# Group 4 of the modulation weights: from TensorE products to VectorE sums, behind the attention units of a fused transformer front

## The reference

```python
sc, sc_ctx = silu(c), silu(c_ctx)
for i in range(2):
    m  = (sc     @ w_mod[i] + b_mod[i]).reshape(1, 6, 1024)   # w_mod[i]: 1024 x 6144
    mc = (sc_ctx @ w_mod[i] + b_mod[i]).reshape(6, 1024)
    sh1, s1, g1, sh2, s2, g2 = ...                            # used as x * (1 + s1) + sh1, and so on

merged = sigmoid(g_a) * (out_a @ w_proj_a) + sigmoid(g_b) * (out_b @ w_proj_b)
mix = merged @ w_out
x = layer_norm(ALPHA * x + mix)          # then the router and the experts
```

## Time and profile before

| what | value |
|---|---|
| median of 3 runs | 3478.19 us (3475.61 to 3481.51) |
| profiled execution | 3470.34 us, span of the profile 3468.5 us |
| TensorE busy | 3156.0 us (91%), mean granted clock 0.985 |
| VectorE, ScalarE, GpSimd busy | 1831.5 us (53%), 1130.2 us (33%), 882.6 us (25%) |
| transfers | 1366.35 MB, mean 394 GB/s |
| chain that ended last | indirect row transfers 10%, TensorE 9%, VectorE 2% of the span |

### The profile page before, as it was taken

How to read it: one execution, slowest core, us unless ns; L and a number is a source line. 1 busy time by engine, 2 the same in 40 slices (tenths; PEclk the granted TensorE clock), 3 DMA queues, 4 the chain that set the end, 5 groups by cost and what they waited for, 6 DMA issues and landing times. The chain is left out here.

```text
span 3468.5 us, 33334 instructions
## 1 busy us (share of the span) xinstructions
PE 3156.0 (91%) x11076; PEld 1414.2 (41%) x11076; DVE 1831.5 (53%) x4099; ACT 1130.2 (33%) x3024; POOL 882.6 (25%) x798
## 2 busy tenths in 40 slices
PE   9999999999999997989989879889888998987777
PEld 7565333433334432434344323333333643532222
DVE  7743102111221127676776677667765378667665
ACT  1331111110111113444443544555433334444333
POOL 0000000000000003444444444345442034444432
PEclk9999999999999999999999999999999999999999
DMA  9847999999999999999999999999998379999997
GB/s 406 362 175 297 425 425 428 425 423 428 417 427 427 401 427 399 410 422 419 417 421 413 421 411 422 413 412 415 416 421 343 127 309 421 422 421 418 420 421 331
DMA packets 155595, 1366.35 MB, mean 394 GB/s; under 512 B 18341, under 2 KB 18853, under 8 KB 24090
## 3 DMA queue, kind: packets, MB, share of 16 engines
q0 software_dynamic: 111360, 805.46, 56.2%
q1 hardware_dynamic: 44058, 558.70, 38.5%
HBM read 1362.94 MB, written 1.15 MB: 393 GB/s over the span
## 5 line engine op out<-in xcount | busy, mean ns | idle before, releaser
L3423 PE MATMUL ps<-sb_arena,sb_diag 128*128 128x512 f32 x3072 | 1472.7, 619 | 259.4 <-ACT sb_diag L3402 257.4
L1910 POOL DMA_INDIRECT sb_arena<-in_uv,sb_idx x768 | 866.2, 1128 | 2165.1 <-PE ps L3423 1035.5
L3358 DVE SCALAR_TENSOR_TENSOR sb_arena<-sb_arena,sb_H 128x1024 f32<-128x1024 f32 x768 | 941.0, 1226 | 583.5 <-DMA sb_arena<-in_uv,sb_idx 399.2
L3423 PEld LDWEIGHTS ps<-sb_arena,sb_diag 128*128 128x128 f32 x3072 | 563.5, 194 | 1117.6 <-ACT sb_diag L3402 557.6
L1571 PE MATMUL ps<-sb_ring,sb_arena 128*64 128x512 f32 x3072 | 675.2, 595 | 7.4 <-DMA sb_ring<-in_moe 7.4
L3391 ACT ACTIVATE sb_act<-sb_dots 128x1 f32<-128x1 f32 x768 | 154.8, 202 | 998.2 <-DVE sb_arena L3358 993.3
L1571 PEld LDWEIGHTS ps<-sb_ring,sb_arena 128*64 128x64 f32 x3072 | 214.1, 137 | 447.0 <-issue 429.6
L1772 DVE TENSOR_SCALAR sb_arena<-ps 128x512 f32<-128x512 f32 x32 | 22.1, 692 | 585.3 <-PE ps L1571 569.9
L3402 ACT ACTIVATE sb_diag<-sb_consts,sb_act 128x128 f32<-128x128 f32 x768 | 308.4, 402 | 26.1 <-PE ps L3423 1.2
L3397 ACT ACTIVATE sb_act<-sb_act,sb_wts 128x1 f32<-128x1 f32 x768 | 226.2, 295 | 25.0
L183 PE MATMUL ps<-sb_ring,sb_arena 128*128 128x512 f32 x256 | 111.4, 593 | 1.6 <-DVE sb_arena L857 1.3
(11 more groups left out here) (444 smaller groups left out, 2595.5 us busy)
## 6 DMA issues: line engine op xcount, KB each, us to landing
sb_ring<-in_moe SPq DMA_DIRECT2D x192, 2048.0 KB, 17.1
sb_ring<-in_w_mod SPq DMA_DIRECT2D x24, 2048.0 KB, 15.2
sb_ring<-in_w_in SPq DMA_DIRECT2D x10, 2048.0 KB, 15.4
sb_ring<-in_a_w_in SPq DMA_DIRECT2D x8, 2048.0 KB, 14.6
sb_ring<-in_w_q SPq DMA_DIRECT2D x6, 2048.0 KB, 12.7
sb_arena<-in_uv,sb_idx POOLq DMA_INDIRECT x768, 14.4
sb_ring<-in_b_w_in SPq DMA_DIRECT2D x6, 2048.0 KB, 7.8
sb_ring<-in_a_w_out SPq DMA_DIRECT2D x4, 2048.0 KB, 14.4
```

The source lines that it names most:

```text
L1910: pool.indirect_dma_start(row_buffer(m, n), None, d[f"uv{layer}"], bass.IndirectOffsetOnAxis(m.idx[:, pair % 2, k:k + 1], 0))\
L3358: nc.vector.scalar_tensor_tensor(out=u, in0=u, scalar=1.0, in1=m.H[:, order[i], :], op0=ALU.mult, op1=ALU.mult, accum_out=m.dots[:, n_ % P ...
L3423: last = nc.tensor.matmul(out[h], m.diag[n_ % DIAGS], uv[b][:, D + h * 512:D + (h + 1) * 512], start=opens, stop=ends)
```

## The change

Group 4 goes to VectorE. `SUMMED_QUARTERS` becomes a table with all four quarters of group 4 in it. Its two sums lie in the part of the arena that held queries, keys and values ("behind"). `add` becomes a generator, `added`, which stops after every instruction, so that its 16 instructions can be put between others: VectorE runs five steps of it after the last attention unit (the first quarter and one instruction), one after each of the first seven merged tiles, and the last four behind the eighth. TensorE drops `mod.tensor(pe, MOD_END)` ahead of the projections and runs `mod.reduce(pe, MOD_END)` between x1 and x2. The group's bank is now 3 and not 4, ScalarE's copy of it comes behind the first square root of the norm, and SyncE waits for the full bank before it loads the expert biases, whose place overlaps one of the sums.

```diff
@@ -36,7 +36,7 @@
...
 N_MOD = 2 * 6 * D // (4 * 512)
 LATE_MODS = 1
-SUMMED_QUARTERS = (4, 4, 3)
+SUMMED_QUARTERS = {0: 4, 1: 4, 2: 3, 4: 4}
 MOD_FILL, MOD_END = 3, 4
@@ -280,7 +280,11 @@
...
         self.sums = [[m.part(7168, 2048), m.part(9216, 2048)],
                      [m.X[:, 0:2, :].rearrange("p a b -> p (a b)"), m.H[:, 2:4, :].rearrange("p a b -> p (a b)")]]
-        self.where, self.adds = {}, 0
+        self.behind = [m.part(2048, 2048), m.part(5120, 2048)]
+        self.where, self.adds, self.summed = {}, 0, {i: n + 1 for n, i in enumerate(SUMMED_QUARTERS)}
+
+    def sums_of(self, i):
+        return self.behind if i == MOD_END else self.sums[i % 2]
@@ -305,17 +309,21 @@
...
     def add(self, dve, i, quarter):
+        for _ in self.added(dve, i, quarter):
+            pass
+
+    def added(self, dve, i, quarter):
...
         if i == 0 and quarter == 0:
             dve.wait_ge(M("silu_ready"), 1)
-        if i >= 2 and quarter == 0:
+        if i == 2 and quarter == 0:
             self.banks.wait_full(dve, self.where[i - 2])
...
         for k in range(2):
             for stream in range(2):
-                out, scale = self.sums[i % 2][stream], self.silu_c[:, 2 * quarter + k, stream:stream + 1]
+                out, scale = self.sums_of(i)[stream], self.silu_c[:, 2 * quarter + k, stream:stream + 1]
                 if self.adds >= 2:
@@ -324,10 +332,13 @@
...
                 ins.then_inc(M("mod_add"), 1)
                 self.adds += 1
+                if k == 0 or stream == 0:
+                    yield
         dve.wait_ge(M("mod_add"), self.adds)
...
         if quarter == SUMMED_QUARTERS[i] - 1:
             dve.sem_inc(M("mod_summed"), 1)
+        yield
@@ -341,12 +352,12 @@
...
                                             w[:, k, g * 512:(g + 1) * 512], start=False, stop=False, skip_group_check=True)
             self.ring.used(last, name)
-        pe.wait_ge(self.M("mod_summed"), i + 1)
+        pe.wait_ge(self.M("mod_summed"), self.summed[i])
         select = m.const("stream").rearrange("p (s c) -> p s c", s=2)
...
             for g in range(4):
                 last = nc.tensor.matmul(m.ps[32 * g:32 * g + 2, where[0], :], select[:, stream, :],
-                                        self.sums[i % 2][stream][:, g * 512:(g + 1) * 512], start=False, stop=stream == 1,
+                                        self.sums_of(i)[stream][:, g * 512:(g + 1) * 512], start=False, stop=stream == 1,
                                         skip_group_check=True)
@@ -443,12 +454,12 @@
...
     mod.plan([MOD_FILL], [7])
     gg.update(banks.plan([("gate", n) for n in range(2, 8)], [7]))
-    mod.plan([MOD_END], [4])
     pieces = [("gate", n, third) for n in range(8) for third in range(3)]
...
     gm = banks.plan([("m", i) for i in range(KT)], [0, 1, 2, 3, 5, 6, 7, 4])
     gx = banks.plan([("x", i) for i in range(4)], [4, 5, 6, 7])
+    mod.plan([MOD_END], [3])
     router = Router(nc, d, m, M, banks)
@@ -487,6 +498,7 @@
...
             ring.load(sp, ring.at["moe0.0"] + 2)
             sp.wait_ge(M("y_ready"), 2 * TT)
+            banks.wait_full(sp, mod.where[MOD_END])
             router.rest(sp)
@@ -645,7 +657,6 @@
...
-            mod.tensor(pe, MOD_END)
             wa = ring.wait(pe, "w_proj_a", 0)
@@ -668,6 +679,8 @@
...
             for i in range(4):
                 t, half = i // 2, i % 2
+                if i == 2:
+                    mod.reduce(pe, MOD_END)
                 w = ring.wait(pe, "w_out", half)
@@ -762,11 +775,10 @@
...
                     gates_out(n)
             for i in range(4):
-                if i == 2:
-                    mod.scalar(act, MOD_END)
                 for n in (i, 4 + i):
                     nc.scalar.activation(pair_of(n), pair_of(n), ACT.Sigmoid).then_inc(M("gates_ready"), 1)
             norm_act(nc, act, m, M, n0 + 1)
+            mod.scalar(act, MOD_END)
             router.turned(act, 0)
@@ -848,6 +860,9 @@
...
             both = m.part(7168, 2, KT, T)
+            behind = (step_ for quarter in range(4) for step_ in mod.added(dve, MOD_END, quarter))
+            for _ in range(5):
+                next(behind)
             for i in range(KT):
@@ -856,6 +871,10 @@
...
                 nc.vector.tensor_tensor(gates[:, i, :], tmp[:, 0, :], tmp[:, 1, :], ALU.add).then_inc(M("merged_ready"), 1)
                 dve.wait_ge(M("merged_ready"), i + 1)
+                if i + 1 < KT:
+                    next(behind, None)
+            for _ in behind:
+                pass
             dve.wait_ge(M("x_in"), 16)
```

## The result

The changed kernel takes 3481.22 us (median of 20 runs, 3473.76 to 3487.47), the kernel before 3477.31 us in the same comparison (20 runs). The ratio is **1.0016, 95% interval 1.001 to 1.0022**: 3.5 to 7.7 us slower, 5.6 in the middle (the two medians lie 3.9 us apart). The forecast was 1.3 us slower, range -5 to +8. Direction and range held, and the ratio is within the 0.2% that counted as no change; the size forecast was a quarter to a third of the measured one.

The account below looks back on a forecast made before the run. TensorE paces the front; at 424.7 us the nearly full weight stream decides. TensorE gains 8.3, pays 2.9, loses the remaining 5.4 and 1.3 more; 1.3 on the median of 3478.19 gives 3479.5 us, range 3473 to 3486.

Parts of the forecast that it names:

- C, the clock: After TensorE's pause ahead of the first turn the clock falls: 1.9 us, up to 5.3 at both waits; 3482, chance 0.12.
- The removed and added TensorE time: Ahead of the projections 8.3 us go, reduce between x1 and x2 adds 2.9; TensorE has 5.4 us less to do.
- VectorE in step with the tiles: In the merge, tile plus accumulating instruction takes 3.5 us, as TensorE's tile does; w_out starts 7.4 us earlier.
- the ring's hidden loads: Weight loads waiting for VectorE's quarters: w_proj_b's second half hidden by 5.6 us, w_out's second half just in time.
- The rows behind three chunks: The layer norm's rows queue behind w_mod20 to w_mod22, 6 MB, and land at 298.6 in place of 281.9.
- What is late next: Before the first expert: second normalized tile at 311.4, 1.9 us late; first expert 0.5 to 1.5 us later than 322.49.
- The stream: Weight transfers behind w_mod20: moe0.2 lands at 322.1 against 320.8, 1.3 us late, and the stream is full until 424.7.
- A cover of 2.6 us: Near 425 us, a wait of 1.25 us plus the stream's 1.3 absorbs TensorE's own lateness of 0.5 to 1.5.
- a first wait for expert chunks that is gone: Sign of being wrong; the forecast had this wait near 425 us still there, ending near 426.
- Rivals A and B: A: rows in time, 5.4 us reach the end, 3472.8, chance 0.1. B: queue shares bandwidth, rows at 306.5, 3486, chance 0.06.
- Theory 3: Put up for the experiments, not in the prediction: VectorE's sums have a cost that no wait shows; no size given.

Follow-up runs that it names:

- e1: Changed kernel with the layer norm's rows issued at about 232 us, ahead of everything that waits for the sums; ratio 1.0001 to the kernel before.
- e9: Changed kernel with the layer norm's rows issued right behind the wait for the merged tiles, ahead of w_mod20 to w_mod22; ratio 1.0003 to the kernel before.
- e3: Changed kernel with four extra products filling TensorE's pause between x3 and its first turn; ratio 1.0012 to the kernel before.
- e4: Kernel before, with the layer norm's rows, router_w, router_b and ctx issued early; ratio 0.9996 to the kernel before.

## Why the prediction was right, and what it mis-sized

The forecast said that TensorE's 5.4 us are lost on the late rows and the late weights, and a little more; that happened. Its time, 3479.5, held because the range was wide and 0.2% counted as no change: both prices in it were too small, that of TensorE's lateness at the first expert and that of the stream's, and of its cases C, the clock, with 3482 and a chance of 0.12, lies closest to what the traces show.

*The removed and added TensorE time.* 8.3 and 2.9 us: removed as said; reduce took 1.04 and 1.90. But TensorE was only 3.8 us ahead at x3, not 4.7 (299.7 for 304.4): w_out started at 269.36 and not at 268.7, with a wait of 0.27 for w_proj_b and 1.61 for the last merged tile ahead of it.

*VectorE in step with the tiles; the ring's hidden loads.* Right: the last tile was merged at 269.3 (forecast 268.6), the fourth quarter ended at 278.5 (277.9), and no product with w_out waited for its weights. w_proj_b's second half was hidden, as said (landed at 246.8); the wait of 0.27 was for its first.

*The rows behind three chunks.* Right to 0.2 us: VectorE started at 298.79, forecast 298.6. e1 and e9 show that the place of the rows is the cause of the slowdown. It works in two ways, by the pause of a TensorE that is ahead and by the stream, and no run gives the share of each: e3 takes the pause away alone and is not told from the changed kernel, e9 takes it away together with 2.4 us of the stream.

*What is late next.* The second tile was ready at 311.6 (forecast 311.4). Here is the first term that was mis-sized: "The first expert starts 0.5 to 1.5 us later than 322.49". It was 3.9 us on the average of three traces each. The sum had TensorE's second turn held by the tile, at 311.4; in fact TensorE, at half clock, came to it only at 315.85. The low clock is rival C, which had a chance of 0.12 and a price of 1.9 us, taken from 8 matmuls, that "nearly fits into the cover"; it lasted 10 to 14 us in all three traces and took 3 us more than the kernel before's own spells (e3). In the row it was priced by it had lasted 3.4 us (1518.4 to 1521.8), in products of 128x128 by 512. Here turns, logits of 32 columns and products for 2 columns came behind the pause. Whether that is why it lasted longer no run tests.

*The stream.* "1.3 us late" was 5 (moe0.2 at 325.5 to 326.0, before 320.2 to 320.7). Up to moe0.0 the sum held: by it moe0.0 lands at 311.2, and it landed at 311.4 (311.9 and 312.4 in the other two traces). From there moe0.2 needed 13.1 to 14.3 us, where the sum had 10.9. What lies between, besides two chunks, are the expert biases, three transfers of 128 KB, which the sum priced by their size at 1 us; while they ran, the window 316:318 above shows the transfer engines busy (a share of 1.16) and only 211 GB/s moved. So 2 to 3.5 us were missing, and the biases are what the traces show there; no run leaves them out. SyncE's late issue of moe0.2, behind a slow TensorE, is not the reason: in e3 it was issued 2.4 us earlier and landed no earlier. "Issued transfers of one queue land one after another" held for the chunks and the rows, not for the biases: the first of them, issued at 311.63, landed at 317.4, ahead of moe0.1 (issued at 300.75, landed at 319.2).

*A cover of 2.6 us.* It was read from one trace: at the wait of 1.25 us near 425 us the second trace of before has 0.98, and the third has no wait for a chunk until 1016. And the prediction's own sign of being wrong, "a first wait for expert chunks that is gone", came true: in all three traces of the changed kernel TensorE waits for no chunk until 1019.7 at the earliest. So the delay did not go to the end by the path that was forecast, TensorE on time and the stream late, but by a TensorE later than the stream: 4 us at the first expert, and the second low spell on top in two traces. That the stream stands close behind was right: e9 and e3 bring TensorE earlier, and there it waits 4.1 and 2.5 us for chunks. The second spell is by its trace no doing of the pause; whether the change makes it more frequent (two traces of three, none of three before, but four of the eight others) is open.

*Rivals A and B* did not happen: rows landed behind three chunks (A), and not with ctx and w_mod23 (B, whose own sum, up to 9.5 less 1.25, gives 8.2 and not 7.8).

*Theory 3* is open. Against it speak the timed runs: the kernels with VectorE's sums and rows in time are at 0.9992 to 1.0003. For it speaks the lookup stage (span less first lookup product), which was 2141 to 2145 us in the traces of before and 2147 to 2149 in those of the changed kernel, and over all fourteen traces 2147 on average with the sums (eight, 2142 to 2149) and 2144 without (six, 2141 to 2145). That is 3 us with no wait named for it, and nothing was run to find its cause.

## What to carry to other kernels

When work is moved to another engine, ask who frees the buffers now: here SyncE's in-order waits turned a slot freed 39 us later into a small transfer that came 17 us late, behind 6 MB nobody needed yet. Put the small load that is wanted next ahead of the big ones that are wanted later. An engine that is made faster without its inputs gains a pause, and here the pause cost some 3 us more than its length, in a longer spell of the low clock. And a margin between two engines that are nearly level, read from one trace, is no margin: here it was 1.2 us, 1.0 us or nothing in three traces of one kernel.

## What the runs showed of the hardware that I had not expected

The granted clock fell to 0.50 with TensorE busy in every window (before, second trace: 308.8 to 312.2 us; e1: 303.8 to 310.7; e9: 305.5 to 308.9), each time in the same stretch of turns, logits and group 5's products, and in some traces of one kernel and not in others. The same stretch of work took 17.8, 19.4, 21.0 or up to 23.3 us by it; a second such place, at 346 to 361 us, has a spell in 6 of 14 traces: 6.8 us of low clock in five, worth 3.3 us where it was measured, and 3.4 us in one (e4). Two places like these make a scatter of several microseconds between runs of one kernel, as large as the effect that was to be measured.

Three transfers of 128 KB (the expert biases) came with 2 to 3.5 us more of the stream's time than their bytes make at 425 GB/s, by the landings in the changed kernel's three traces, and two of them (landed at 317.4 and 318.3 in the first) overtook a 2 MB chunk that the same engine had issued 11 us earlier (319.2).
